# Closing normalisation reordered, inverse transform in other PSUM banks, in a two-layer Hyena and neighbourhood-attention step

## What is computed

```python
def bidir_long_conv(v, k_fwd, k_bwd, bias):
    ...
    kf = jnp.fft.rfft(k_circ, axis=0)
    vf = jnp.fft.rfft(v.astype(jnp.float32), n=2 * L, axis=1)
    y = jnp.fft.irfft(vf * kf[None], n=2 * L, axis=1)[:, :L]
    return (y + v.astype(jnp.float32) * bias).astype(v.dtype)
...
for i in range(DEPTH):
    ...
    xs = layer_norm(ALPHA * xs + g1_s * os_, ln1_g[i], ln1_b[i])
    ...
    fs = swiglu(xs * (1.0 + sc2_s) + sh2_s, ffn_w_in[i], ffn_w_out[i])
    ...
    xs = layer_norm(ALPHA * xs + g2_s * fs, ln2_g[i], ln2_b[i])
```

## Time and profile before

| | us |
|---|---|
| median of three runs | 3791.66 (3787.71 to 3795.18) |
| the profiled execution, its own time | 3793.69 |
| span of the profiled execution | 3791.9 |
| PE busy | 3603.6 |
| DVE busy | 1523.5 |
| POOL busy | 1230.1 |
| ACT busy | 1033.7 |

### The profile page before, as it was taken

The page is one execution under the profiler, slowest core; times in us unless marked ns, Lnnn a source line. Parts: engine busy times, 40 slices in busy tenths (PEclk is TensorE's granted clock), DMA queues, the critical chain, the costliest instruction groups (busy, mean ns, idle before and its releaser), DMA issues. The chain is left out here.

```text
span 3791.9 us, 47285 instructions
## 1 busy us (share of the span) xinstructions
PE 3603.6 (95%) x19244; PEld 3074.2 (81%) x19244; DVE 1523.5 (40%) x2472; ACT 1033.7 (27%) x1552; POOL 1230.1 (32%) x813
## 2 busy tenths in 40 slices
PE   8999998989999999999989998999899999999997
PEld 6788887768788888888868877888778888888885
DVE  2775553664334444344441014777240222111116
ACT  1441111232511111111252224777343111111113
POOL 1531113633422222222361214666253222222223
PEclk9999999999999999999989998999999999999998
DMA  3253323744122222222243456776201111111111
GB/s 118 87 168 119 106 91 132 255 150 156 43 64 70 81 67 73 67 67 67 67 161 128 152 176 164 178 174 158 84 29 39 34 39 39 39 39 34 39 39 61
DMA packets 173366, 365.38 MB, mean 96 GB/s; under 512 B 16839, under 2 KB 98247, under 8 KB 171496
## 3 DMA queue, kind: packets, MB, share of 16 engines
q1 hardware_dynamic: 167720, 352.01, 29.2%
q10 hardware_dynamic: 5440, 10.49, 0.9%
HBM read 284.84 MB, written 77.59 MB: 96 GB/s over the span
## 5 line engine op out<-in xcount | busy, mean ns | idle before, releaser
L148 POOL TENSOR_TENSOR w_lo<-w_raw,w_hi 128x1024 fp32r<-128x1024 f32 x207 | 501.7, 2424 | 1487.1 <-ACT w_hi L142 1487.1
L156 PE MATMUL ps_r<-a_hi,w_hi 128*128 128x512 f32 (+1 forms) x2496 | 643.8, 360 | 17.1 <-POOL a_lo L1796 9.8
L156 PE MATMUL ps_r<-a_lo,w_hi 128*128 128x512 f32 (+1 forms) x2496 | 638.7, 358 | 0.0
L156 PE MATMUL ps_r<-a_hi,w_lo 128*128 128x512 f32 (+1 forms) x2496 | 638.2, 357 | 0.0
L156 PEld LDWEIGHTS ps_r<-a_hi,w_hi 128*128 128x128 f32 x2496 | 417.3, 189 | 100.8 <-POOL a_lo L1796 17.6
L142 ACT ACTIVATE w_hi<-w_raw 128x1024 fp32r<-128x1024 f32 x207 | 217.7, 1052 | 989.7 <-PE ps_r L156 567.0
L156 PEld LDWEIGHTS ps_r<-a_lo,w_hi 128*128 128x128 f32 x2496 | 417.3, 189 | 74.7 <-issue 1.8
L156 PEld LDWEIGHTS ps_r<-a_hi,w_lo 128*128 128x128 f32 x2496 | 416.9, 189 | 74.2
L1989 DVE TENSOR_TENSOR hid_l<-hid_l,ps_r 128x1280 f32<-128x1280 f32 x44 | 65.5, 1488 | 843.6 <-PE ps_r L156 843.6
L2009 DVE SCALAR_TENSOR_TENSOR x_t_l<-ps_r,mod,x_t_l 128x1024 f32<-128x1024 f32 (+1 forms) x288 | 241.4, 880 | 266.0 <-PE ps_r L156 266.0
L1836 POOL TENSOR_TENSOR hid_lo_l<-hid_l,hid_hi_l 128x1280 fp32r<-128x1280 f32 x42 | 134.6, 3205 | 491.3 <-ACT hid_hi_l L1737 491.3
(11 more groups left out here) (249 smaller groups left out, 6060.0 us busy)
## 6 DMA issues: line engine op xcount, KB each, us to landing
w_raw<-in_w_all SPq DMA_DIRECT2D x213, 512.0 KB, 3.6
ada_w_l<-in_ada_t SPq DMA_DIRECT2D x59, 512.0 KB, 3.5
v_hl<-v_d SPq DMA_DIRECT2D x128, 128.0 KB, 2.9
t_tail_f<-in_ada_t SPq DMA_DIRECT2D x24, 512.0 KB, 4.1
spec<-gout_f SPq DMA_DIRECT2D x80, 128.0 KB, 2.1
g_spec_c<-spec ACTq DMA_DIRECT2D x20, 512.0 KB, 4.6
v_d<-z_v_l SPq DMA_DIRECT2D x10, 1024.0 KB, 4.9
q_hl_l<-q_d SPq DMA_DIRECT2D x32, 320.0 KB, 6.7
```

What stands on the lines that cost most here:

```text
L148: pool.tensor_tensor(wl[:, s, 0:width], raw[:, s, 0:width], wh[:, s, 0:width].bitcast(F32), ALU.subtract).then_inc(w_split, 1)
L156: last = pe.matmul(out[:, c0:c1], w[:, c % 2, blk * 128:blk * 128 + 128], x[:, c0:c1], start=start and b == 0 and term == 0, stop=stop and ...
```

## The change

Four edits. (1) `pi` is laid out so that block 0 lies in the banks of columns 0 and 1024, block 1 in those of 512 and 1536; PE waits for `pr_ok` 17 before block 0, and for 18 only before block 1. (2) ACT splits entries e0 + 4 and e0 + 5 ahead of the context's first copy; before, they came behind it and behind the next block's copy. (3) For the last chunk of n2, the small matmuls write to a bank of `pg[1]` and are issued before the wait for `xn`; they count `stat_e`, on which DVE's `variance` now waits. DVE normalises the last four tiles of chunk 1 after the last `add_square`; ACT and POOL follow in that order, and ACT's root of the last chunk stands before the last two of these tiles. (4) In layer 1 DVE makes the modulation coefficients after the accumulations of the first six output tiles, no longer before the first.

```diff
--- before.py
+++ after.py
@@ -785,7 +785,7 @@
             yc_h = nc.alloc_sbuf_tensor_at("y_ctx_hi", [128, 4, 1024], F32R, offset=base_a + 49152).ap()
             y67 = nc.alloc_sbuf_tensor_at("y_raw67", [128, 2, 256], F32, offset=base_a + 65536).ap()
             pf = [st.enter_context(nc.psum_tensor(f"ps_fw{g}", [128, 2048], F32)) for g in range(2)]
-            pi = [[pf[0][:, 1024 * g + 512 * j:1024 * g + 512 * j + 512] for j in range(2)] for g in range(2)]
+            pi = [[pf[0][:, 512 * g + 1024 * j:512 * g + 1024 * j + 512] for j in range(2)] for g in range(2)]
             pc = pf[1]
             x2_h = nc.alloc_sbuf_tensor_at("w2_hi", [128, 2, 1024], F32R, offset=base_a + 67584).ap()
             x2_l = [nc.alloc_sbuf_tensor_at(f"w2_lo{j}", [128, 1024], F32R, offset=base_a + (75776, 0)[j]).ap() for j in range(2)]
@@ -934,13 +934,16 @@
                     else:
                         act.wait_ge(ya, c)
                     act.activation(an[:, :], pi[c % 2][1], ACT.Copy).then_inc(an_ok, 1)
+                    if c >= 2:
+                        split_hi(act, e0 + 2 * c + 3)
                     if c:
-                        split_hi(act, e0 + 2 * c + 3)
                         act.wait_ge(al_ok, c)
                     else:
+                        split_hi(act, e0 + 4, used=e0 + 1)
+                        split_hi(act, e0 + 5, used=e0 + 2)
                         act.wait_ge(c_mm, 1)
                     act.activation(yt[:, LS:TOK], pc[:, 256 * c:256 * c + 256], ACT.Copy).then_inc(yp_ok, 1)
-                    if c < 7:
+                    if 1 <= c < 7:
                         split_hi(act, e0 + 2 * c + 4)
                     act.wait_ge(g_ok, c + 1)
                     act.activation(a_h[:, c, :], yt[:, :], ACT.Copy).then_inc(ah_ok, 1)
@@ -1046,7 +1049,7 @@
                     return last
 
                 pe.wait_ge(bl_ok, 8)
-                pe.wait_ge(pr_ok, 18)
+                pe.wait_ge(pr_ok, 17)
                 for j in range(2):
                     pe.wait_ge(w_split, e0 + j + 1)
                     inverse(0, j, range(6))
@@ -1058,6 +1061,8 @@
                         pe.wait_ge(w_split, e0 + 2 * c + j + 1)
                         if c >= 2:
                             pe.wait_ge(an_ok if j else ya, c - 1)
+                        if c == 1:
+                            pe.wait_ge(pr_ok, 18)
                         last = second(j) if c == 1 else inverse(c, j, range(8))
                         last.then_inc(w_used, 1)
                         if c == 1 and j == 1:
@@ -1383,7 +1388,7 @@
                 xs_ok, coef1, coef2, xa_ok, y_out = [sem(n, st) for n in ("xs_ok", "coef1", "coef2", "xa_ok", "y_out")]
                 silu, gated, hh_ok, hl_ok, out_mm, out_ok = [
                     sem(n, st) for n in ("silu", "gated", "hh_ok", "hl_ok", "out_mm", "out_ok")]
-                hl_e = sem("hl_e", st)
+                hl_e, stat_e = sem("hl_e", st), sem("stat_e", st)
                 cb_in, cb_ok, aw_in, ad_ok, aw_in2, ad_ok2, md_ok, md_r = [
                     sem(n, st) for n in ("cb_in", "cb_ok", "aw_in", "ad_ok", "aw_in2", "ad_ok2", "md_ok", "md_r")]
                 aw_in = [aw_in, sem("aw_in1", st)]
@@ -1509,13 +1514,18 @@
                         done = adds(ln, pos(ln, 7, ci)) + 1
                         pe.wait_ge(ln.s1_ok, done)
                         pe.wait_ge(ln.s2_ok, done)
-                        if ci:
+                        last = ln is n2 and ci == 2
+                        if ci and not last:
                             pe.wait_ge(ln.xn, 8 * ci)
+                        small = pg[1] if last else px
                         for v, s in enumerate((s1, s2)):
                             for n in range(tiles):
                                 o = 512 + 2 * (v * tiles + n)
-                                pe.matmul(px[:, o:o + 2], s[:, c0 + 128 * n:c0 + 128 * n + 128], meanw[:, 0:2],
-                                          start=True, stop=True)
+                                ins = pe.matmul(small[:, o:o + 2], s[:, c0 + 128 * n:c0 + 128 * n + 128], meanw[:, 0:2],
+                                                start=True, stop=True)
+                        if last:
+                            ins.then_inc(stat_e, 1)
+                            pe.wait_ge(ln.xn, 8 * ci)
                         pe.matmul(px[:, 0:c1 - c0], meanw[:, :], s1[:, c0:c1], start=True, stop=True).then_inc(ln.stat, 1)
 
                     def spread(ln, ci):
@@ -1753,6 +1763,12 @@
                                 split_hi(act, e + 2 + j, r, 12)
                     rounds(step_in, step_out)
 
+                    def end_part(ci, ks):
+                        if last_layer:
+                            final(ci, ks)
+                        else:
+                            modulate(n2, ci, ks)
+
                     for ci in range(3):
                         for m in range(8):
                             square(n2, m, ci)
@@ -1762,16 +1778,13 @@
                                 root(n2, ci - 1)
                             if ci == 1 and m == 3 and not last_layer:
                                 act.wait_ge(coef2, 5)
-                            if ci and m >= 4:
-                                if last_layer:
-                                    final(ci - 1, range(2 * m - 8, 2 * m - 6))
-                                else:
-                                    modulate(n2, ci - 1, range(2 * m - 8, 2 * m - 6))
+                            if ci == 1 and m >= 4 or ci == 2 and m in (4, 5):
+                                end_part(ci - 1, range(2 * m - 8, 2 * m - 6))
+                    end_part(1, range(4, 6))
                     root(n2, 2)
-                    if last_layer:
-                        final(2, range(8))
-                    else:
-                        modulate(n2, 2, range(8))
+                    end_part(1, range(6, 8))
+                    end_part(2, range(8))
+                    if not last_layer:
                         qkv_act(act)
 
                 @block.gpsimd
@@ -1846,9 +1859,10 @@
                     for ci in range(3):
                         for m in range(8):
                             add_x(n2, m, ci)
-                            if ci and m >= 4 and not last_layer:
+                            if not last_layer and (ci == 1 and m >= 4 or ci == 2 and m in (4, 5)):
                                 low(n2, ci - 1, range(2 * m - 8, 2 * m - 6))
                     if not last_layer:
+                        low(n2, 1, range(4, 8))
                         split_lo(pool, eq)
                         split_lo(pool, eq + 1)
                     if not last_layer:
@@ -1882,8 +1896,12 @@
 
                     def variance(ln, ci):
                         w = width(ln, ci) // 64
-                        dve.wait_ge(ln.stat, ci + 1)
-                        dve.tensor_copy(cm[:, 0:2 * w], px[:, 512:512 + 2 * w]).then_inc(ln.cst, 1)
+                        if ln is n2 and ci == 2:
+                            dve.wait_ge(stat_e, 1)
+                        else:
+                            dve.wait_ge(ln.stat, ci + 1)
+                        small = pg[1] if ln is n2 and ci == 2 else px
+                        dve.tensor_copy(cm[:, 0:2 * w], small[:, 512:512 + 2 * w]).then_inc(ln.cst, 1)
                         dve.wait_ge(ln.cst, 4 * ci + 1)
                         dve.tensor_tensor(cv[:, 0:w], cm[:, 0:w], cm[:, 0:w], ALU.mult).then_inc(ln.cst, 1)
                         dve.wait_ge(ln.cst, 4 * ci + 2)
@@ -1927,9 +1945,8 @@
                                                      op0=ALU.mult, op1=ALU.add,
                                                      accum_out=acc_a[:, n, q:q + 1]).then_inc(done, 1)
 
-                    if layer == 1:
-                        dve.wait_ge(xs_ok, KT)
-                    modulation(dve, coef1, layer, SC2, SH2, 4 * layer)
+                    if layer == 0:
+                        modulation(dve, coef1, layer, SC2, SH2, 4 * layer)
                     for m in range(6):
                         for ci in range(3):
                             if ci == 0:
@@ -1943,6 +1960,8 @@
                                 dve.wait_ge(aw_in[n % 2], 16 * (n // 2) + 16)
                                 ada_row(n, (aw, aw2)[n % 2], cb0, ad_ok)
                     dve.wait_ge(xs_ok, KT)
+                    if layer == 1:
+                        modulation(dve, coef1, layer, SC2, SH2, 4 * layer)
                     if layer == 0:
                         dve.wait_ge(ad_ok, 16)
                         dve.tensor_tensor(mod[:, 40:48, :], acc_a[:, 0:8, :],
@@ -2024,9 +2043,11 @@
                                 variance(n2, ci - 1)
                             if ci and m == 2:
                                 inverse(n2, ci - 1)
-                            if ci and m >= 4:
+                            if ci == 1 and m >= 4 or ci == 2 and m in (4, 5):
```

(2 more changed lines are left out.)

## The result

| | before | after |
|---|---|---|
| median | 3789.45 us (five runs, 3785.25 to 3795.18) | 3767.94 us (five runs, 3763.5 to 3771.4) |
| profiled execution, its own time | 3793.69 | 3763.66 |
| its span | 3791.9 | 3761.9 |

The ratio is 0.9943, with a 95% interval of 0.9929 to 0.9957: 21.5 us faster (16 to 27). The profiled execution after is 30 us shorter than the profiled one before; part of that is chance of the two executions, as the experiments show.

The account below looks back on a forecast made before the run. PE, busy 3603.6 of 3791.9 us, was taken as the bound, so only its holes and half clock count. Terms 6.9 + 5.4 + 10.4 - 1.1 + 4.9 = 26.5 us gave a median of 3765.2, range 3755 to 3779.

Parts of the forecast that it names:

- inverse transform: Whole inverse transform stage, first blocks and third block together: 6.9 us gained, bounds 4.5 to 8.1.
- First blocks: Inverse transform, blocks 0 and 1: first hole closes, most is given back at the next entry; 1.5 us gained (0.6 to 2.2).
- Third block: Inverse transform, third block: wait of 4.3 us goes, with 1.4 of half clock, less 0.3 for a late next entry.
- End of layer 0: Layer 0's closing statistics: cache split 4.0 us earlier, plus 1.4 of half clock before second query weight; 5.4 us (2.0 to 8.7).
- Start of layer 1: Layer 1's start: hole and half clock go, 10.4 us, less 1.1 (0 to 2.5) for moved coefficients delaying the row sums.
- End of layer 1: Layer 1's closing statistics: small matmuls run during DVE's pairs, variance and root beside the mean; 4.9 us (3.4 to 6.9).
- (a): Rival: half clock eats more, 5.6 us behind the hole at 740, all kept behind 1979; 3767.5 us, chance 0.25.
- (b): Rival: no PE stop before layer 0's second query weight, since the cache load decides, not POOL; 3762 us, chance 0.2.
- (c): Rival: layer 1's start gain is hidden by ACT's squares behind its splits; 17 us gained, 3775 us, chance 0.1.
- (d): Rival: nothing of note anywhere, moved waits come back everywhere; within 7 us, chance 0.05.
- (e): Rival: slower, POOL's new order in layer 0 delays query products and cache transfers if ACT's root is late; 3800, chance 0.03.

Follow-up runs that it names:

- part alone: Kernel before with only the edits acting on that stretch: e3 (ratio 0.9992) for the transform, e2 (0.9959) for both layer ends, e1 (0.9981) for layer 1's start.
- e9: The whole changed kernel run again, unaltered, against the kernel before: 3764.48 us against 3787.82, ratio 0.9931.
- e3: Kernel before with only the inverse transform's edits, new bank layout with earlier start and earlier splits: 3783.53 us, ratio 0.9992.
- e5: Kernel before with only the new banks and earlier start of block 0: 3789.95 us beside 3787.19, one execution each.
- e10: Changed kernel plus three moves: coefficients behind third output tile, one entry split earlier, POOL's first query split earlier; 3764.61 us, ratio 0.9936 against the kernel before.
- e6: Kernel before with only the entries' splits moved ahead of the context's copy: 3787.66 us beside 3787.19, one execution each.
- e1: Kernel before with only layer 1's modulation coefficients moved behind the first six output tiles: 3780.47 us against 3787.49, ratio 0.9981.
- e2: Kernel before with only the closing normalisation of both layers changed (early small matmuls and new order): 3772.51 us, ratio 0.9959.
- e4: The kernel before once more, with no edit, for the spread of the stretches: one run, 3779.82 us.

## Why the prediction held, and which terms were off

The forecast was 26.5 us and 3765.2; measured were 21.5 us (16 to 27) and 3767.9 beside the first comparison, and 23.3 us and 3764.5 in the second. By stretches, forecast, the changed kernel's two traces with the part alone, and their mean:

| | forecast | part alone, after, e9 | mean |
|---|---|---|---|
| inverse transform | 6.9 | 6.2, 5.4, 2.1 | 4.6 |
| end of layer 0 | 5.4 | 5.6, 5.7, 5.9 | 5.7 |
| start of layer 1 | 9.3 | 6.2, 8.6, 8.7 | 7.8 |
| end of layer 1 | 4.9 | 4.9, 4.9, 4.9 | 4.9 |
| sum | 26.5 | | 23.0 |

- **First blocks, 1.5.** The mechanism held: the hole moved on to block 1, because its entries wait for no one on PE. The hole there was 3.10 (forecast 3.3) with 3.4 us of half clock (forecast 3.3). What the prediction passed over is that DVE's product of the first half waits for a load of the spectrum too: in after 1.05 us of the first hole stayed. By pieces the gain was 0.6 us in after, 1.4 in e3, 0.1 in e5, 2.3 in e10 and -2.8 in e9. The bounds of 0.6 and 2.2 were too narrow for what two loads and the clock do here.
- **Third block, 4.3 + 1.4 - 0.3.** The hole and its half clock went: 4.5 us, and 2.2 us of clock against the mean of the traces that keep the hole (1.4 was that of the one trace of before). "It may be up to 1 us late, I take 0.3 off" was the term that was mis-sized: with PE's two waits of 0.62 and 0.77 the time from the start of block c = 2 to that of c = 4 is 1.9 us longer than at full pace. I had named DVE's long operations beside POOL's split, but priced them as a delay of one entry; they stretched POOL's 2.4 us to 3.72, and the next entry was late too. e10 took back 0.9 of it. The two errors partly cancel, which was luck: 4.7 by pieces (4.9 in e6's stretch) for 5.4.
- **End of layer 0, 4.0 + 1.4.** Near in both terms: the second query weight came 4.0 us earlier (48.04 into the stretch, 52.1 in the mean), and behind it 1.6 us of half clock were gone. The hole shrank to 0.99, not 2, for PE came to it later than forecast. POOL's chain stood where I had it: the last chunk's low parts took 10.64. Of the half clock all went and not half; but in five of the six traces that keep the hole it lasted 3.4 us or less and not the 5.6 of rows 2, so all of it was worth 1.6 and not 2.8: the term came out by luck in part.
- **Start of layer 1, 10.4 - 1.1.** The hole went, and PE did not stand still for the first accumulation. The moved block cost 1.11 us in after and 1.10 in e1 and e9, as forecast. The Trainium skill, SBUF — State Buffer, section Who interferes with whom, has it that a VectorE instruction with two SBUF inputs and a GpSimd one that reads SBUF lock each other out until the first is through; the trace agrees, to 0.03 us, but the price was paid once and not by each of the three instructions of that kind, as POOL's run of adds ended before the others. The clock was somewhat over-sized: 2.55 us was taken from the one trace of before, and the mean of the eight traces that keep the hole is 2.2. That trace, 169.99, is at the slow end of 166.4 to 170.1, and half clock is why: it passed 23.9 us of this stretch at half clock, and the fastest (e2), with no less idle time, 10.2. The 6.2 of e1 is small for the same reason.
- **End of layer 1, 3.4 to 6.9, taken 4.9.** Right to a tenth, in four traces (e2, after, e9, e10). Nothing behind it hides anything. The clock does not matter: half clock lasted to the end in after and e9, and 6.8 us in e2 and e10, with stretches of 24.14 to 24.17.
- **The rivals.** (a) did not come true in after: half clock behind 740 lasted 3.4 us, as the forecast had it, and none came behind 1965. (b) nearly did, with 0.99 and 0.95 us of PE's wait left, though POOL and not the cache load held the second weight; the load joins in only in e10. (c), the start hidden anyway, (d) and (e) are refuted; POOL's changed order cost PE nothing, since its first query product was reached at 1934.28, 1.2 us earlier counted from the last product of layer 0.

What stays open is when a hole of some 3 us is followed by half clock, and why the ratio of e2 is larger than its stretches.

## What to carry to other kernels

Follow each closed hole to the next entry, load or split on the same queue before pricing it: here a hole of 4.3 us was worth some 1 us, and the same kind of hole, where what came next was ready, all of its length. Where two edits each remove one of two waits for the same event, measure them together; apart they gave 2.0 and -0.8 us, together 4.9. And before a term is taken from one trace, look at how much the same stretch differs in a second execution of the same kernel: at the start of layer 1 that was 3.7 us, as much as a whole edit. Where a stretch shows no gain, cut it shorter, with the time at half clock beside each piece, before the move is called useless: two moves of e10 gave 1.1 and 1.4 us at their own place and nothing in their stretch.

## What the runs showed of the hardware

- Matmuls back to back at a granted clock of 1.00 ran at two paces some 0.5% apart: the ffn of layer 1 (with at most 3.4 us at half clock in it) took 912.6 to 912.9 us in ten executions and 907.9 to 908.0 in two (e4, the unchanged kernel, and e3). The difference is spread evenly: the same 460 matmuls took 89.48 and 88.97 us. It did not go with the kernel, and the cause is open; it is as much as a whole term of the sum.
- Holes of 0.95, 0.99 and 1.46 us before the second query weight were followed by no half clock; holes of 3.15 to 4.74 there were, for 3.4 or 6.8 us. Before block 1 a hole of 3.10 was followed by 3.4 us of it and one of 3.28 (e10) by none. At the start of layer 1 the number and length of the spells differed between executions with the same holes, 10.2 to 23.9 us in all.
- An instruction of DVE of 0.17 us took 0.93, 1.15, 1.19 and, before, 1.72 when it had two inputs in SBUF and POOL was at work. Two long ones met one after the other: a POOL split begun 0.08 us after such a DVE instruction of 1.55 us took 3.72 in place of 2.4, and the next DVE instruction, begun while the split ran, 3.56 in place of 1.49.
- The stretch before the transform, which no edit touches, took from 716.9 to 725.6 us in twelve executions.
